# Operands 8 and 32 bytes off a multiple of 128: an on-chip layout change in a kernel of float32r products

## What is computed

```python
# first block: gated linear attention (HGRN2) in both directions, then a mixture of 16 experts, 2 active
mod = silu(c) @ w_mod + b_mod
h = modulate(x, g, shift, scale)                  # rms norm, gain, shift
q, v, zf, zb, g = split(h @ w_in, 5)              # 8 heads of 128, chunks of 64
x = x + g1 * ((readout of both scans) @ w_out)
y = y + combine[:, e:e+1] * ((silu(h @ w_gate[e]) * (h @ w_up[e])) @ w_down[e])
# second block, two layers:
def swiglu(x, w_gu, w_d):                         # d_ff = 2816, four times in all
    gate, up = split(x @ w_gu, 2)
    return (silu(gate) * up) @ w_d
# layer 0 mixes by differential attention and RWKV-7, layer 1 by retention with 4 heads
```

## Time and profile before

| | us |
|---|---|
| median of 3 runs | 3111.27 |
| lowest, highest | 3108.0, 3115.29 |
| the profiled execution | 3112.57 |
| its span, first to last instruction | 3110.8 |
| TensorE products, busy | 3023.7 (97%) |
| VectorE, busy | 2130.3 (68%) |
| ScalarE, busy | 1527.0 (49%) |
| mean granted TensorE clock | 0.991 of 2.4 GHz |

### The profile page before, as it was taken

One profiled execution on the slowest core, in us unless ns is written; L12 is line 12 of the kernel. 1 busy time (PEld: TensorE's weight loads), 2 busy tenths in 40 slices (PEclk: granted clock), 3 DMA queues, 4 the chain that ended last, 5 costly groups with the idle time before them and its releaser, 6 DMA issues.

```text
span 3110.8 us, 49298 instructions
## 1 busy us (share of the span) xinstructions
PE 3023.7 (97%) x19037; PEld 2567.9 (83%) x19037; DVE 2130.3 (68%) x3065; ACT 1527.0 (49%) x2263; POOL 67.2 (2%) x115
## 2 busy tenths in 40 slices
PE   7999999899999999998999999999999999999998
PEld 3888887788779897767878989789988787779996
DVE  5576666899878586775578867786864443588685
ACT  4454645677645354563245534554543332455452
POOL 1000000000000000300000000000000000000000
PEclk9999999899999999999999999999999999999999
DMA  5222222799823232210013323232222222223221
GB/s 225 89 76 79 76 81 83 274 379 380 318 70 121 95 109 86 68 56 18 24 61 108 109 96 108 82 122 102 102 95 83 80 82 81 75 76 121 102 102 68
DMA packets 97101, 354.81 MB, mean 114 GB/s; under 512 B 10896, under 2 KB 11280, under 8 KB 96528
## 3 DMA queue, kind: packets, MB, share of 16 engines
q1 hardware_dynamic: 92448, 334.54, 30.5%
q0 software_dynamic: 3168, 11.54, 1.0%
q10 hardware_dynamic: 1296, 6.11, 0.5%
HBM read 344.27 MB, written 7.86 MB: 113 GB/s over the span
## 4 chain that ended last, share of the span: by engine, by line
PE 89%; DVE 5%; ACT 4%; issue 1%; DMA 1%; POOL 0%; SPq 0%; ACTq 0%; DVEq 0%; POOLq 0%
PE bank L353 13%; PE bank L355 13%; PE bank L354 13%; PE bank L961 7%; PE bank L963 7%; PE bank L962 7%; PE bank L2812 2%; PE bank L2814 2%; PE bank L2813 2%; PE bank L557 1%; PE bank L558 1%; PE bank L562 1%; PE cbank L379 1%; PE bank L3969 1%; PE gbank L1646 1%
## 5 line engine op out<-in xcount | busy, mean ns | idle before, releaser
L325 ACT ACTIVATE whi<-raw 128x1024 fp32r<-128x1024 f32 x310 | 319.2, 1050 | 219.5 <-PE bank L355 182.4
L344 DVE TENSOR_TENSOR wlo<-raw,whi 128x1024 fp32r<-128x1024 f32 x310 | 375.5, 1222 | 71.1 <-ACT whi L325 70.3
L353 PE MATMUL bank<-h_hi_buf,whi 128*128 128x512 f32 x1008 | 409.7, 406 | 8.2 <-DVE h_lo_buf L493 5.1
L355 PE MATMUL bank<-h_hi_buf,wlo 128*128 128x512 f32 x1008 | 394.5, 391 | 0.0
L354 PE MATMUL bank<-h_lo_buf,whi 128*128 128x512 f32 x1008 | 394.0, 391 | 0.0
L353 PE MATMUL bank<-a_hi_buf,whi 128*128 128x512 f32 x832 | 324.9, 391 | 0.5 <-DVE wlo L344 0.5
L354 PE MATMUL bank<-a_lo_buf,whi 128*128 128x512 f32 x832 | 323.8, 389 | 0.0
L355 PE MATMUL bank<-a_hi_buf,wlo 128*128 128x512 f32 x832 | 323.7, 389 | 0.0
L353 PEld LDWEIGHTS bank<-h_hi_buf,whi 128*128 128x128 f32 x1008 | 189.9, 188 | 54.7 <-DVE h_lo_buf L493 6.8
L355 PEld LDWEIGHTS bank<-h_hi_buf,wlo 128*128 128x128 f32 x1008 | 189.7, 188 | 41.3
L354 PEld LDWEIGHTS bank<-h_lo_buf,whi 128*128 128x128 f32 x1008 | 190.1, 189 | 40.1 <-issue 4.1
(11 more groups left out here) (724 smaller groups left out, 7251.9 us busy)
## 6 DMA issues: line engine op xcount, KB each, us to landing
raw<-in_w SPq DMA_DIRECT2D x622, 512.0 KB, 4.4
held<-in_w SPq DMA_DIRECT2D x12, 512.0 KB, 16.5
x<-in_x ACTq DMA_DIRECT2D x2, 2048.0 KB, 11.1
sorted_y<-ysb POOLq DMA_DIRECT2D x6, 512.0 KB, 7.7
token_rows<-hrow POOLq DMA_DIRECT2D x4, 512.0 KB, 4.3
out<-x SPq DMA_DIRECT2D x8, 256.0 KB, 2.0
xc<-in_xc ACTq DMA_DIRECT2D x1, 1024.0 KB, 8.7
sorted_y<-zrow POOLq DMA_DIRECT2D x1, 512.0 KB, 3.1
```

Of the source, the lines that this page charges most:

```text
L325: act.activation(weights(k, g)[0], k.raw[:, g.slot, :], ACT.Copy).then_inc(k.split_hi, 2 * RING + 1 if first == COND_GROUPS * RING else 1)
L344: dve.tensor_tensor(lo, k.raw[:, g.slot, :], hi.bitcast(F32), ALU.subtract).then_inc(k.split_lo, 2 * RING + 1 if first == COND_GROUPS * RI ...
L353: pe.matmul(out, w_hi, hi, start=(t == 0), stop=False)
L355: return pe.matmul(out, w_lo, hi, start=False, stop=(t == tiles - 1))
```

## The change

The two weight rings become one tensor with 8 bytes more; the cut that is `whi` starts 8 bytes into it, and `wlo` follows directly, so it is 8 bytes behind a multiple of 128 too. The offset is then raised to the next multiple of 128 for `h_hi_buf` and `h_lo_buf`, which thereby move by 128 bytes. 32 bytes are left out before `a_hi_buf`, so that it and all that follows or is placed after `k.low` and `k.top` (`x`, `acc`, `hc`, `sums`, `sum_hi`, `mix_hi`, `whi2`, `wlo2`, `raw2` and the rest) move by 160 bytes, and what was on a multiple of 128 is 32 behind one. What is laid over `h_hi_buf` and `h_lo_buf` (the experts' `xs_hi`, `at_hi` and others) stays on multiples of 128. `raw` doesn't move. No instruction, shape, wait or order changes.

```diff
+        def both_halves_behind(name, shape, names, skew):
+            n = int(np.prod(shape[1:]))
+            begin = at
+            t = bump(name, [P, 2 * n + skew // 4], F32R)
+            for b, half in enumerate(names):
+                arena[half] = (begin + 4 * n * b, begin + 4 * n * (b + 1))
+            cut = lambda b: t[:, skew // 4 + b * n:skew // 4 + (b + 1) * n].rearrange("p (c f) -> p c f", c=shape[1])
+            return cut(0), cut(1)
@@
         k.raw = bump("raw", [P, RING, D])
-        k.whi = bump("whi", [P, RING, D], F32R)
-        k.wlo = bump("wlo", [P, RING, D], F32R)
+        k.whi, k.wlo = both_halves_behind("weight_halves", [P, RING, D], ("whi", "wlo"), 8)
+        at = -(-at // 128) * 128
         k.h_hi_buf = bump("h_hi_buf", [P, DC, T], F32R)
         k.h_lo_buf = bump("h_lo_buf", [P, DC, T], F32R)
+        at += 32
         k.a_hi_buf = bump("a_hi_buf", [P, DC, T], F32R)
```

## The result

| | before | after |
|---|---|---|
| median | 3112.44 us (4 runs) | 3144.73 us (4 runs) |
| lowest, highest | 3108.0, 3115.29 | 3143.1, 3146.72 |
| the profiled execution's span | 3110.8 | 3145.0 |
| TensorE products, busy | 3023.7 | 3065.0 |
| TensorE's mean granted clock | 0.991 | 0.989 |

The changed kernel is slower: ratio 1.0103, interval [1.0088, 1.0118]. 3045 was forecast with a range up to 3135, so sign and range were both wrong. (An interval in square brackets is the 95% interval of the ratio to the kernel before.)

A forecast was written before the change was run, and what follows sets the result against it. TensorE's pace of product starts was taken as the bound. 42 us (512 wide) plus 36 (256 wide) make 78, of which 85%, 66 us, off 3112.6 gives 3046.5, set to 3045 for the median; range 2990 to 3135.

The forecast's parts named there:

- What bounds the kernel: Whole kernel: TensorE, busy 97% of the span, sets the time through the distance between starts of its products.
- the left-over: Full-rate float32r products: 13.3 ns beyond the columns' time, said to depend on operand places, in steps of 6.67 ns.
- rival 1: All products: nothing happens, the 13.3 ns being a fixed price of a full-rate read; 3111 us, chance 0.18.
- the premise on the pairs: Moving/stationary places modulo 128: all 0/0 before; after, 0/8, 32/8, 0/32 and 32/32, with h_hi_buf and h_lo_buf at 0.
- term one: 6324 512-wide products outside the experts: pace down one step of 6.67 ns, 226.7 to 220.0, 42 us less.
- Term two: 5376 256-wide products at L961 to L963: pace down one step of 6.67 ns, 120.0 to 113.3, 36 us less.
- The 85% that arrive: Of the 78 us gained on 512- and 256-wide products, 85% was taken to reach the time: 66 us.
- What is next in line: Behind a quicker TensorE: VectorE still fits in seven-pass tiles; DMA limits the experts, whose weight products were credited with nothing.
- Rival 4: Slower: 512- and 256-wide products lose 226.7 and 120.0, experts lose too; up to 3176 us, chance 0.20, half below 3130.
- Term three: ScalarE and VectorE at shifted addresses: nothing taken, within 8 ns either way, 1.3 us at most over 168 expert blocks.
- Term four: Expert-stage DMA with raw2 at 32 modulo 128: nothing taken, up to 12 us kept for the range.
- Rival 2: Part of it: only one kind of pair, h or a against weights, gets quicker; 17 to 45 us, 3080, chance 0.17.

The follow-up runs named there:

- e11: The changed kernel with the offset behind the weight halves rounded up to a multiple of 256 instead of 128, both skews kept: 3125.65 us, ratio 1.0040 to the kernel before.
- e9: Small TensorE-only kernel, 48 products per pair, moving places up to 512 and stationary up to 256 bytes behind a multiple of 2048: 226.7 ns at 0/0, 232.5 at 128/0.
- e7: The kernel before with only 128 bytes left out ahead of h_hi_buf, no skew: 3145.31 us, ratio 1.0090.
- e10: The kernel before with 128 bytes left free ahead of the weight halves, so weights, h, a, mixes and sums all move: 3113.3 us, ratio 0.9998.
- e2: The changed kernel without the 32 bytes before a_hi_buf, the 8-byte weight skew kept: 3142.17 us, ratio 1.0094 to the kernel before.
- three grids: Small kernels e1, e4 and e9, which leave out the whole computation and time 48 TensorE products per pair of moving/stationary places; lowest 512-wide pace 226.7 ns.
- e4: Small TensorE-only kernel, both operands' places in steps of 16 bytes modulo 128, then only the moving low half shifted: 512 wide 226.7 ns at 0/0; low half shifted 231.3 to 235.6.
- e1: Small TensorE-only kernel, fifty pairs of moving/stationary places modulo 128, 48 products each: 512 wide, the stationary place alone moves the pace from 226.7 to 234.3 ns.
- e6: The kernel before with only the sums and mixes of the seven-pass tiles starting 64 bytes later: 3104.0 us, ratio 0.9969.

## Why the prediction was wrong, point by point

**What bounds the kernel: right.** TensorE's pace is the time. 34.5 us of start distances make 34.2 us of span, no wait was added, and edits of nothing but addresses moved the end by -10 to +32 us. The prediction held the 2.5 ns of the Trainium skill ("TensorE: Matmul & The Clock Gate", section "Back-to-back issue gap") against the trace's 13.3; in that section the 2.5 ns are those of an isolated product, so the two aren't quite the same quantity. That doesn't enter the sum.

**That the left-over depends on places, in steps of 6.67 ns: right.** 226.7 became 233.3, and 120.0 became 113.3 where a pair allowed it. The argument from the earlier trace rows that the 13.3 ns are no fixed price of an instruction stands; rival 1, nothing happens, was wrong for the reason given there.

**Two steps of the prediction failed, and they can be priced apart.** Forecast were -66 us and measured +32. e11 has the very pairs that the prediction assumed and is at about +12. So some 80 us of the miss belong to the value of the terms, one step of 6.67 ns down, and the other 20 to the premise on the pairs. The value alone makes the sign wrong.

**The premise "before, all are 0/0 modulo 128, after it 0/8, 32/8, 0/32, 32/32": wrong.** The period is 256 (e9). The text on the change notes that h moves by 128 bytes, and the prediction put h at 0 as if nothing had happened to it. This move is the part that costs most: alone it gives 1.0090 (e7), the relation restored gives 0.9998 (e10), and the weights' skew of 8 on top of it adds nothing that can be told (e2: 1.0094). The period of 128 had been inferred from the earlier trace rows as "the time of 16 or 32 columns, which are 64 or 128 bytes"; a step in time was turned into a period in address, and no row could show that, because every operand before stood on a multiple of 512.

**The value of term one, one step down: wrong in sign, and wrong even for the pairs meant.** For 6324 products -42 us was taken. Measured are +37.5 us with the parked blocks' and L557 to L562's products. At the pairs that the text had in mind, e11 has 230.6 and about 231, a loss too. Of all pairs in three grids none is below 226.7 by more than the reading error of 0.1. The reason given, that a start only 0.11 us behind another occurs in the earlier trace rows, was weak: a single short distance behind a long one is part of an unsettled pattern and says nothing of a rest. The nearest row to the truth was the worst bound, 231.7 ns; the measured 233.3 is 1.6 ns beyond it, so the bound was also too tight.

**Term two, the 256-wide products, one step down:** right in sign, mis-sized. -36 us was taken, -7.8 came (650.9 to 643.1 us), since 113.3 belongs to few pairs and since these stages change pairs every 12 products.

**The 85% that arrive:** not tested by itself; for the a/weights products 6.5 of 6.67 ns arrived, 97%, for h/weights 4.9, 73%; I suppose because runs with h are interrupted more often: a mean distance before of 718.9 / 3024 = 237.7 ns against a's 227.8.

**What is next in line:** didn't come up, since nothing got quicker. The experts' products of weights, credited with nothing, cost 5.2 us more in after; e10, which should equal the kernel before, has 1.0 more there, so most of it can be taken as real. Rival 4's 3 us for these products were near.

**Term three, the other engines at shifted addresses: right.** L325 1050 to 1051 ns, L344 1222 to 1224 ns. **Term four, the transfers: right** to take nothing, though the sign that was named for it, 379 GB/s unchanged, didn't come (373): the longer window has the same fall to 362 GB/s in after and in e7, whose `raw2` stands on a multiple of 128. The estimate of some 7 us more that the text worked out from the Trainium skill ("DMA: Bandwidth & Descriptors", section "How a descriptor splits into AXI transactions") isn't seen: the expert products cost 5.2 us more in after and 3.8 in e7, which leaves 1.4 us for the skew of all operands together.

**Rival 4 is what happened** for the 512-wide products: the rest at 226.7 was lost because the stationary and the moving operand no longer stood to each other as before. Its reason in full was not right. It was the 128 bytes between them, not the 8, that cost most; an equal place is neither enough for 226.7 (16/16) nor needed (0/120); the 256-wide products got quicker, not slower; and its pace wandering about 231.7 didn't come: in after it settles, one step higher. It had a chance of 0.20 and half of it lay outside the range. The one upper bound that rows supported belonged to this rival, and no row at all supported a 512-wide pace of 220; that should have decided the order of the chances.

**Rival 2's price** was added up too low: two of its three parts (24, 17 and 36 us) make up to 60, not 45. It changes nothing here.

**Open:** why a given relation has the pace it has. The grids show the period, the paces and the settling, not what in the two reads meets every 6.67 ns. Nor do they say why some pairs have two paces.

## What to carry to other kernels

Back-to-back float32r products have a pace that depends on where the moving operand stands to the stationary one modulo 256 bytes; before skewing anything, know the period, and when operands stand well to each other now, move them together, by a multiple of 32 bytes, when an array ahead of them grows. When a layout edit changes sizes, write down every address that it moves, round-ups included, and test "only the round-up" first. A pace from a microbenchmark holds for long runs of one pair; where pairs change every dozen products, expect part of it.

## What the runs showed that was not expected

- The pace depends on both operands' places modulo 256 bytes: 0/0 and 128/128 226.7 ns, 0/128 232.2 and 128/0 232.3 (e9). Shifting both by 32 keeps it in nearly all cases, by 16 it doesn't: 0/0 226.7, 16/16 233.3 (e4). A shift of only the low half of the moving operand is enough to lose 226.7 (231.3 to 235.6, e4).
- 226.7 ns is the floor for 512 columns over all pairs tried, but 113.3 for 256 columns, 6.7 over the columns' 106.7, where 0/0 has 13.3 over. So the best place differs with the width: 0/64 is at 113.3 and 233.2.
- Settling takes a few products, and not always as many: in e9's first pass 256/0 rests after two distances (233, 230, then 227 on) and 128/128 after four (236, 229, 232, 231), and 0/0 in its second pass after seven (241, 224, 231, 236, 228, 233, 230). 0/8 never rests but repeats 234, 230, 231, 229, 229.
- Some pairs have two paces: 0/16 is at 233.3 in e1 and at 226.7 in e4, and in e1's two passes 32/48 is at 226.7 and at 233.3. What ran before a pair thus plays a part; how, wasn't tested.
- In e9, after 24.4 us in which TensorE was idle, products 2 to 10 start 427 ns apart: 512 columns at 1.2 GHz (426.7) with nothing left over. The views print a granted clock of 1.00 there, but the trace's own rows of the clock begin only 28.5 us into the span, where the quicker starts begin. The left-over of 13.3 ns is seen at the upper level alone.
- 64 bytes in front of the sums made the tuned kernel 0.31% faster (e6: 3104.0 us), with no instruction changed.
